# Placing the split weights 16 bytes further on in SBUF, in a two-block float32 transformer kernel

## The chip, the cores and the metric

The kernel runs on one core of a Trainium2 chip. Its time is the device time of one execution in microseconds (us). Lower is better. Three executions were timed.

## The reference

`reference()` computes two blocks on one sequence of 512 tokens and width 1,024, all in float32. The parts that fill the time are the linear layers:

```python
proj = u @ w_in                                   # first block, 1024 -> 2840
h = h + rmsnorm(mixed @ w_out, norm_mix_post)
qx = hn @ w_q_x;  kx, vx = jnp.split(mn @ w_kv_x, 2, axis=-1)
h = h + rmsnorm(ox @ w_o_x, norm_x_post)
g, up = jnp.split(hn @ w_gate_up, 2, axis=-1)     # 1024 -> 2 x 2816
h = h + rmsnorm((silu(g) * up) @ w_down, norm_ffn_post)
...
for l in range(2):                                # second block, two layers of the same kind
    proj = einsum(h, w_in[l]);  ...;  x = x + einsum(merged, w_out[l])
    x = x + (silu(g) * up) @ w_down[l]
```

Between them stand the first block's three attention branches (compressed, selected, window) with a short convolution, a cross-attention to 256 memory tokens, and in each of the two layers of the second block a sliding-window attention with a 31-tap convolution.

## The kernel before

Activations are kept transposed: a tile such as `x_hi` [128, 8, 512] holds feature chunk `k` in its partitions and the 512 tokens along them. Every float32 product of a linear layer is made of three products in `fp32r`, a float32 format that TensorE takes in one pass. Both operands are split in a high part, rounded to fp32r, and a low part, the rest; high x high, low x high and high x low are summed in PSUM. `products` (L406 to L417) issues these three:

```python
pe.matmul(dst, wh[:, k, cols], hi[:, kx_, at:at + width], start=start, stop=False)   # L415
pe.matmul(dst, wh[:, k, cols], lo[:, kx_, at:at + width], start=False, stop=False)   # L416
return pe.matmul(dst, wl[:, k, cols], hi[:, kx_, at:at + width], start=False, stop=stop)  # L417
```

The weights (128 columns) are the stationary operand and are loaded by a weight load (`LDWEIGHTS`, engine PEld) ahead of each matmul. The activations are the moving operand, 512 columns wide, or 256 where a stage works on half the tokens or on the 256 memory tokens. In `tokens_major` (L506 to L516) it is the other way round: the activations are loaded and the weights move, 256 columns wide.

The weights come as a stream of 183 units of 128 x 2048 float32 (8 KiB per partition). Three slots take turns. For each unit SyncE issues a DMA into `w_raw` (L662), ScalarE copies it rounded into `w_hi` (`split_hi`, L293 to L297), VectorE writes `w_raw - w_hi` into `w_lo` (`split_lo`, L299 to L302), and TensorE runs its 48 matmuls. ScalarE waits for the matmuls of the unit three before (`unit_done`), VectorE for ScalarE (`hi_ready`), TensorE for VectorE (`lo_ready`), and the DMA of a slot for VectorE's reading of it. The order of each engine's work is written out by hand.

The attention stages use plain float32 matmuls (for example `kx,qx` at L1570), in which no tile of this stream takes part. Two small stages use fp32r with a narrower stationary operand: the gates (L836 to L838, 24 columns of `wg_hi`/`wg_lo`, moving `x_hi`/`x_lo`), and the compression (L877 to L879, 62 columns of `xc_hi`/`xc_lo`, moving `w_hi`/`w_lo`).

**Places in SBUF.** `place` (L110 to L115) gives each tile a start in the partition and moves a cursor on by the tile's size, rounded up to 32 bytes. L130 rounds the cursor up to 128 bytes ahead of the weights:

```python
where[0] = (where[0] + 127) // 128 * 128
w_raw = place("w_raw", [P, SLOTS, UNIT])
w_hi = place("w_hi", [P, SLOTS, UNIT], F32R)
w_lo = place("w_lo", [P, SLOTS, UNIT], F32R)
h = place("h", [P, DT, T])
```

After them come `h`, `x_hi`, `x_lo`, `rbc`, `acc`, `sq`, and then a region (`scope`) that each stage lays out anew: `f_hi`/`f_lo` of the feed-forward layers, `m_hi`/`m_lo` of the memory, `c_hi`/`c_lo` and `o_hi`/`o_lo` of the second block. Their sizes are multiples of 512 bytes, and L212 pads the region so that `cy` (and with it `c_lo`, `o_hi`, `o_lo`) also starts a multiple of 512 bytes from `scope`. So the distance from `w_hi` or `w_lo` to the start of each of x, f, m, c and o, high and low, is a multiple of 512 bytes. Inside the tiles the steps are such multiples too: 2,048 bytes from chunk to chunk of the activations, 1,024 (or 2,048) bytes and 512 bytes inside a unit. Only the narrow operands differ: `wg_hi` and `wg_lo` are read in steps of 96 bytes, `xc_hi` and `xc_lo` start at 96 bytes past a multiple of 128 and are read in steps of 248 bytes. A line of 16 bytes holds four float32.

Of the kernel before, what the change touches and what calls it, by code (L numbers as in the profile page):

```python
# [23 lines left out]
F32R = mybir.dt.float32r  # L24
# [6 lines left out]
P = 128  # L31
# [16 lines left out]
LOW = -1e20  # L48
SLOTS = 3
UNIT = 2048  # L50


U_IN, U_W1, U_OUT, U_KV, U_QX, U_OX, U_GU, U_DN, U_L = 0, 11, 15, 19, 27, 31, 35, 57, 69
# [47 lines left out]
def build(nc, w, x, mem, pos, pack, tables, cmask, w2, wg, rope2, out):  # L101
    ctx = ExitStack()
    with ctx:
# [6 lines left out]
        def place(name, shape, dt=F32, cursor=where):  # L110
            size = int(np.prod(shape[1:])) * (2 if dt == BF16 else 4)
            t = nc.alloc_sbuf_tensor_at(name, shape, dt, offset=cursor[0])
            cursor[0] += (size + 31) // 32 * 32
            assert cursor[0] <= nc.sbuf_usable_end, (name, cursor[0])
            return t  # L115
# [13 lines left out]
        jcol = place("jcol", [P, 64])  # L129
        where[0] = (where[0] + 127) // 128 * 128  # L130
        w_raw = place("w_raw", [P, SLOTS, UNIT])
        w_hi = place("w_hi", [P, SLOTS, UNIT], F32R)
        w_lo = place("w_lo", [P, SLOTS, UNIT], F32R)
        h = place("h", [P, DT, T])
        act_at = [where[0]]
        y_ffn = place("y_ffn", [P, DT, T], F32, act_at)
# [144 lines left out]

        HALF = UNIT // 2
        QUARTER = UNIT // 4
        FIRST_GAINS = 8
# [2352 lines left out]
def unit_pack(weight, cols, rows=8):  # L2637
# [4 lines left out]
    for c in range(0, k, rows):  # L2642
        u = np.zeros((P, rows, UNIT // rows), np.float32)
        m = min(rows, k - c)
# [114 lines left out]
```

## Time and profile before

| | us |
|---|---|
| median of 3 runs | 2248.32 |
| lowest and highest run | 2246.68, 2249.13 |
| span of the profiled execution, first to last instruction | 2246.4 |
| TensorE busy in it | 2224.9 |
| TensorE weight loads busy | 1821.7 |
| VectorE busy | 1245.1 |
| ScalarE busy | 885.6 |
| GpSimd busy | 280.7 |

The page gives no separate device time for the profiled execution; its span is 1.9 us below the median of the timed runs. Matmuls are pipelined: a matmul's record lasts longer than the distance to the next one's start, so the mean duration of a matmul is not what it costs. What it costs is the distance from start to start, called its pitch below, which is read from the timeline. The granted TensorE clock has two levels, 1.2 and 2.4 GHz. A stream of 512 columns at one column per cycle takes 213.3 ns at 2.4 GHz, one of 256 columns 106.7 ns.

### The profile page before, as it was taken

What the parts mean: (1) busy time and instruction counts of PE and PEld (TensorE: products, weight loads), DVE (VectorE), ACT (ScalarE), POOL (GpSimd) and SP (SyncE); (2) the same over time, 40 slices, a digit from 0 to 9 for tenths busy, and PEclk for the clock granted to TensorE, in tenths of its full rate; (3) what the DMA queues carried; (4) which work ended last, traced back from release to release, by engine and by line L of the source; (5) the groups of instructions that cost most, each with busy time, mean ns of one, the idle gap of its engine ahead of it and who ended that gap; (6) DMA issues with size and microseconds to landing.
All of it is one profiled execution on the core that took longest, in us unless ns stands there. A gap on an engine that the chain in (4) does not pass through costs nothing.

```text
span 2246.4 us, 29245 instructions
## 1 busy us (share of the span) xinstructions
PE 2224.9 (99%) x11388; PEld 1821.7 (81%) x11388; DVE 1245.1 (55%) x1836; ACT 885.6 (39%) x1363; POOL 280.7 (12%) x273
## 2 busy tenths in 40 slices
PE   9999999999999999999999999999999999999999
PEld 7877888898888888886778888888887668888887
DVE  6467656445444225999664444333889664544422
ACT  5545454354333225234744333222323753433321
POOL 3000032011000001014331000001003442000000
PEclk9999999999999999999999999999999999999999
DMA  6221033122222231321122222222221112322222
GB/s 223 100 76 57 20 121 126 55 72 99 103 102 93 94 113 69 113 75 57 56 77 81 107 93 93 100 106 105 104 84 57 39 66 85 113 102 104 94 101 86
DMA packets 30484, 203.19 MB, mean 90 GB/s; under 512 B 3504, under 2 KB 4144, under 8 KB 6704
## 3 DMA queue, kind: packets, MB, share of 16 engines
q1 hardware_dynamic: 29088, 197.34, 24.4%
q10 hardware_dynamic: 1296, 4.46, 0.5%
q8 instruction: 69, 1.13, 0.2%
q14 instruction: 31, 0.25, 0.0%
HBM read 199.69 MB, written 2.10 MB: 90 GB/s over the span
## 4 chain that ended last, share of the span: by engine, by line
PE 93%; DVE 3%; POOL 1%; ACT 1%; issue 1%; DMA 0%; ACTq 0%; DVEq 0%; POOLq 0%
PE bank L415 26%; PE bank L417 26%; PE bank L416 26%; PE bank L2110 1%; PE bank L1002 1%; PE bank L2120 1%; PE bank L2133 1%; PE bank L973 1%; PE bank L2028 1%; POOL acc L324 1%; PE bank L990 1%; PE bank L2010 1%; PE bank L1593 1%; PE bank L1570 1%; PE bank L515 1%
## 5 line engine op out<-in xcount | busy, mean ns | idle before, releaser
L415 PE MATMUL bank<-x_hi,w_hi 128*128 128x512 f32 (+1 forms) x2032 | 789.9, 389 | 5.9 <-DVE x_lo L1766 2.3
L417 PE MATMUL bank<-x_hi,w_lo 128*128 128x512 f32 (+1 forms) x2032 | 775.0, 381 | 0.0
L416 PE MATMUL bank<-x_lo,w_hi 128*128 128x512 f32 (+1 forms) x2032 | 774.1, 381 | 0.0
L301 DVE TENSOR_TENSOR w_lo<-w_raw,w_hi 128x2048 fp32r<-128x2048 f32 x167 | 386.2, 2313 | 412.3 <-ACT w_hi L297 412.3
L297 ACT ACTIVATE w_hi<-w_raw 128x2048 fp32r<-128x2048 f32 x167 | 319.7, 1916 | 585.8 <-PE bank L417 583.9
L415 PEld LDWEIGHTS bank<-x_hi,w_hi 128*128 128x128 f32 x2032 | 382.1, 188 | 83.6 <-issue 6.8
L417 PEld LDWEIGHTS bank<-x_hi,w_lo 128*128 128x128 f32 x2032 | 381.9, 188 | 74.9
L416 PEld LDWEIGHTS bank<-x_lo,w_hi 128*128 128x128 f32 x2032 | 382.4, 188 | 72.7 <-issue 2.9
L415 PE MATMUL bank<-f_hi,w_hi 128*128 128x512 f32 (+1 forms) x572 | 213.3, 373 | 0.0
L416 PE MATMUL bank<-f_lo,w_hi 128*128 128x512 f32 (+1 forms) x572 | 213.2, 373 | 0.0
L417 PE MATMUL bank<-f_hi,w_lo 128*128 128x512 f32 (+1 forms) x572 | 213.2, 373 | 0.0
L2345 DVE SCALAR_TENSOR_TENSOR cy<-la,gains,cy 128x512 f32<-128x512 f32 x240 | 173.9, 794 | 0.0
L563 DVE TENSOR_TENSOR bank<-bank,rbc 128x512 f32<-128x512 f32 x66 | 46.0, 697 | 167.6 <-PE bank L417 159.6
L415 PEld LDWEIGHTS bank<-f_hi,w_hi 128*128 128x128 f32 x572 | 107.7, 188 | 19.0
L416 PEld LDWEIGHTS bank<-f_lo,w_hi 128*128 128x128 f32 x572 | 107.7, 188 | 18.9
L417 PEld LDWEIGHTS bank<-f_hi,w_lo 128*128 128x128 f32 x572 | 107.7, 188 | 18.7
L324 POOL TENSOR_TENSOR acc<-acc,sq 128x512 f32<-128x512 f32 (+1 forms) x48 | 77.6, 1618 | 144.2 <-ACT sq L308 140.4
L552 ACT ACTIVATE f_hi<-bank 128x512 f32 x66 | 39.6, 599 | 115.5 <-DVE bank L569 115.5
L571 DVE TENSOR_TENSOR f_lo<-bank,f_hi 128x512 f32 x66 | 45.7, 692 | 58.4 <-ACT f_hi L552 58.4
L2590 POOL TENSOR_TENSOR lprob<-lprob,small 128x512 f32<-128x512 f32 (+1 forms) x64 | 61.9, 967 | 123.6 <-DVE small L2419 77.8
L2260 ACT ACTIVATE lprob<-lprob,small 128x257 f32<-128x257 f32 (+1 forms) x128 | 60.5, 475 | 31.5 <-DVE small L2415 30.9
L324 POOL TENSOR_TENSOR acc<-sq 128x512 f32<-128x512 f32 (+1 forms) x8 | 14.4, 1801 | 442.8 <-ACT sq L308 442.8
(355 smaller groups left out, 2637.2 us busy)
## 6 DMA issues: line engine op xcount, KB each, us to landing
w_raw<-w_d SPq DMA_DIRECT2D x184, 1024.0 KB, 4.8
out_d<-h SPq DMA_DIRECT2D x8, 256.0 KB, 6.6
h<-x_d ACTq DMA_DIRECT2D x3, 512.0 KB, 9.2
tab<-rope_d ACTq DMA_DIRECT2D x2, 640.0 KB, 3.9
memT<-mem_d ACTq DMA_DIRECT2D x1, 1024.0 KB, 4.8
w_raw<-w_d SPq DMA_DIRECT2D x2, 256.0 KB, 4.1
h<-x_d ACTq DMA_DIRECT2D x2, 256.0 KB, 5.8
w_raw<-w_d SPq DMA_DIRECT2D x1, 512.0 KB, 6.6
```

Of the source, the lines that this page charges most:

```text
L297: act.activation(w_hi[:, u.slot, :], w_raw[:, u.slot, :], ACT.Copy).then_inc(hi_ready, 1)
L301: dve.tensor_tensor(w_lo[:, u.slot, :], w_raw[:, u.slot, :], w_hi[:, u.slot, :], ALU.subtract).then_inc(lo_ready, 1)
L324: pool.tensor_tensor(acc[:, 0:width], sq[:, 0, 0:width] if k == 1 else acc[:, 0:width], sq[:, k % 2, 0:width], ALU.add).then_inc(acc_ready, 1)
L415: pe.matmul(dst, wh[:, k, cols], hi[:, kx_, at:at + width], start=start, stop=False)
L416: pe.matmul(dst, wh[:, k, cols], lo[:, kx_, at:at + width], start=False, stop=False)
L417: return pe.matmul(dst, wl[:, k, cols], hi[:, kx_, at:at + width], start=False, stop=stop)
L552: act.activation(pick(f_hi, j, i), up, ACT.Copy).then_inc(f_hi_done, 1)
L563: dve.tensor_tensor(g, g, rbc[:, :], ALU.mult).then_inc(gu_scaled, 1)
L571: dve.tensor_tensor(pick(f_lo, j, i), up, pick(f_hi, j, i), ALU.subtract).then_inc(f_lo_done, 1)
L2260: act.activation(row, row, ACT.Exp, bias=asm(j, 0, e), scale=-1.0, accum_out=asm(j, 4, e)).then_inc(A["exp"], 1)
L2345: dve.scalar_tensor_tensor(out=cy[:, m, :], in0=src, scalar=wt, in1=cy[:, m, :], op0=ALU.mult, op1=ALU.add).then_inc(l_tap, 1)
L2590: pool.tensor_tensor(row, row, asm(j, 12).unsqueeze(2).to_broadcast([P, 2, 2 * P - c0]), ALU.mult).then_inc(A["scaled"], 1)
```

## The change

`w_hi` and `w_lo` become views of one tile, `w_split`, that begins where `w_hi` began and has four unused float32 (one line of 16 bytes) ahead of them. No instruction is added, removed or moved; only start addresses differ.

```diff
+LINE = 4
...
         w_raw = place("w_raw", [P, SLOTS, UNIT])
-        w_hi = place("w_hi", [P, SLOTS, UNIT], F32R)
-        w_lo = place("w_lo", [P, SLOTS, UNIT], F32R)
+        w_split = place("w_split", [P, LINE + 2 * SLOTS * UNIT], F32R)
+        w_hi, w_lo = (w_split[:, LINE + i * SLOTS * UNIT:LINE + (i + 1) * SLOTS * UNIT].rearrange("p (s c) -> p s c", s=SLOTS) for i in range(2))
         h = place("h", [P, DT, T])
```

`w_hi` and `w_lo` start 16 bytes later than before. `w_split` is 49,168 bytes long, rounded up to 49,184, so that `h` and all tiles after it start 32 bytes later. `w_raw` and what is ahead of it stay. The distance from the split weights to x, f, m, c and o becomes a multiple of 512 bytes plus 16. Distances among the tiles after `w_split` stay as they were, those between `wg_hi`/`wg_lo` and `x_hi`/`x_lo` among them.

## Rows read from the trace of the kernel before

**Rows 1.** The page: span, TensorE's share, and its granted clock in 40 slices.
```profile
span 2246.4 us, 29245 instructions
PE 2224.9 (99%) x11388; PEld 1821.7 (81%) x11388; DVE 1245.1 (55%) x1836; ACT 885.6 (39%) x1363; POOL 280.7 (12%) x273
PEclk9999999999999999999999999999999999999999
```

**Rows 2.** The page's chain that ended last, by engine and by line.
```profile
PE 93%; DVE 3%; POOL 1%; ACT 1%; issue 1%; DMA 0%; ACTq 0%; DVEq 0%; POOLq 0%
PE bank L415 26%; PE bank L417 26%; PE bank L416 26%; PE bank L2110 1%; PE bank L1002 1%; PE bank L2120 1%; PE bank L2133 1%; PE bank L973 1%; PE bank L2028 1%; POOL acc L324 1%; PE bank L990 1%; PE bank L2010 1%; PE bank L1593 1%; PE bank L1570 1%; PE bank L515 1%
```

**Rows 3.** Groups by line and form, TensorE: count | busy us, mean ns | idle before.
```profile
L415 PE MATMUL bank<-x_hi,w_hi 128*128 128x512 f32 x1872 | 743.6, 397 | 3.6 <-DVE w_lo L301 2.0 <-DVE x_lo L406 1.4
L415 PE MATMUL bank<-f_hi,w_hi 128*128 128x512 f32 x484 | 188.3, 389 | 0.0
L415 PE MATMUL bank<-o_hi,w_hi 128*128 128x512 f32 x128 | 51.1, 399 | 0.0
L415 PE MATMUL bank<-x_hi,w_hi 128*128 128x256 f32 x160 | 46.3, 289 | 2.3 <-DVE x_lo L1766 2.3
L415 PE MATMUL bank<-c_hi,w_hi 128*128 128x512 f32 x64 | 27.5, 430 | 0.0
L415 PE MATMUL bank<-f_hi,w_hi 128*128 128x256 f32 x88 | 25.1, 285 | 0.0
L415 PE MATMUL bank<-m_hi,w_hi 128*128 128x256 f32 x64 | 18.3, 285 | 0.0
L514 PE MATMUL bank<-w_hi,m_hi 128*128 128x256 f32 x64 | 18.1, 283 | 0.0
L514 PE MATMUL bank<-w_hi,x_hi 128*128 128x256 f32 x32 | 9.4, 295 | 0.0
```

**Rows 4.** Timeline, TensorE, 512 columns in the feed-forward stage: start us, duration us.
```profile
699.63 0.39 PE L417 MATMUL bank<-x_hi,w_lo 128*128 128x512 f32 x1
...
701.90 0.39 PE L415 MATMUL bank<-x_hi,w_hi 128*128 128x512 f32 x1
```

**Rows 5.** Timeline, TensorE, 256 columns of the down projection.
```profile
829.73 0.28 PE L416 MATMUL bank<-f_lo,w_hi 128*128 128x256 f32 x1
...
830.93 0.28 PE L417 MATMUL bank<-f_hi,w_lo 128*128 128x256 f32 x1
```

**Rows 6.** Timeline, TensorE, plain float32 matmuls of the cross-attention, eight merged.
```profile
404.71 1.89 PE L1570 MATMUL bank<-kx,qx 128*128 128x256 f32 x8
```

**Rows 7.** Timeline, TensorE, 512 columns between attention work in the second block.
```profile
1101.33 0.39 PE L416 MATMUL bank<-c_lo,w_hi 128*128 128x512 f32 x1
...
1103.63 0.39 PE L417 MATMUL bank<-c_hi,w_lo 128*128 128x512 f32 x1
```

**Rows 8.** Timeline, TensorE, the gates: 24 stationary columns, 512 moving.
```profile
74.01 0.39 PE L836 MATMUL bank<-x_hi,wg_hi 128*24 128x512 f32 x1
...
75.85 0.40 PE L838 MATMUL bank<-x_hi,wg_lo 128*24 128x512 f32 x1
```

**Rows 9.** Timeline, TensorE, the compression: 62 stationary columns, 256 moving.
```profile
91.10 0.28 PE L877 MATMUL bank<-w_hi,xc_hi 128*62 128x256 f32 x1
...
92.98 0.28 PE L878 MATMUL bank<-w_lo,xc_hi 128*62 128x256 f32 x1
```

**Rows 10.** The page's groups: the two splits of the weights.
```profile
L301 DVE TENSOR_TENSOR w_lo<-w_raw,w_hi 128x2048 fp32r<-128x2048 f32 x167 | 386.2, 2313 | 412.3 <-ACT w_hi L297 412.3
L297 ACT ACTIVATE w_hi<-w_raw 128x2048 fp32r<-128x2048 f32 x167 | 319.7, 1916 | 585.8 <-PE bank L417 583.9
```

**Rows 11.** The page's DMA issues: KB each, us from issue to landing.
```profile
w_raw<-w_d SPq DMA_DIRECT2D x184, 1024.0 KB, 4.8
out_d<-h SPq DMA_DIRECT2D x8, 256.0 KB, 6.6
h<-x_d ACTq DMA_DIRECT2D x3, 512.0 KB, 9.2
```

## The prediction

> **What bounds the kernel now.** I read the page first. TensorE is busy for 2224.9 of the 2246.4 us and its granted clock is at the upper level, 2.4 GHz, in all 40 slices [rows 1]. The chain that ended last is 93% TensorE, 78% in the three lines of `products` alone [rows 2]. So the kernel is a row of matmuls, and what the change is worth is what it does to their pitch, nothing else of size.
>
> Then I counted the matmuls that read `w_hi` or `w_lo`, from the groups by form [rows 3]. Each of the groups shown stands for three of equal count (high x high, low x high, high x low). With 512 moving columns: (1872 + 484 + 128 + 64) x 3 = 7,644. With 256: (160 + 88 + 64 + 64 + 32) x 3 = 1,224.
>
> Then the pitches, from the timeline; a pitch is the distance of the two starts shown divided by the steps between them.
> - 512 columns, feed-forward: ten steps from 699.63 to 701.90, 227 ns [rows 4]. The stream of columns itself takes 213.3 ns, so 13.7 ns are extra.
> - 256 columns: ten steps in 1.20 us, 120 ns [rows 5], against 106.7: 13.3 extra. The extra does not grow with the columns.
> - Plain float32, the same 128 x 128 weight load ahead of each: eight matmuls in 1.89 us, of which the last lasts 0.38, so seven steps of 216 ns [rows 6]. It streams 256 columns at half the rate, 213.3 ns: 2.7 extra. So a weight load can hide almost fully where the moving operand is read at half the speed.
> - 512 columns right behind attention work: ten steps from 1101.33 to 1103.63, 230 ns [rows 7], by the same instructions at the same distances in SBUF as in rows 4. The pitch has a steady value of 227 and a restless one of 230.
>
> The extra of 11 ns over the float32 case is what the change can reach. 7,644 x 11 + 1,224 x 10.6 = 97 us is all of it, 4.3% of the span.
>
> **The change part by part.** *Removed or added:* no instruction, no wait, no byte of traffic. *Moved:* addresses.
>
> (a) The splits. ScalarE writes `w_hi`, VectorE reads it and writes `w_lo`, at 16 bytes off the old places. 1.92 and 2.31 us per unit [rows 10], both with hundreds of us of idle time ahead, ended by TensorE and by each other: a unit's 48 matmuls take 48 x 0.227 = 10.9 us. Cost 0; it would take a doubling of both to come near that cover, and if the cover went TensorE would wait for `w_lo`. Only the first units lie open: below 1 us either way.
>
> (b) The DMAs. `w_raw` does not move. `h` does, by 32 bytes: its loads (9.2 us to landing) and the eight stores of the result (6.6 us) [rows 11]. Only the last store lies open at the end. If it were a tenth slower or faster that is 0.7 us; I take 0.
>
> (c) The pitch. The trace has no stage with 128 stationary columns and any other distance than a multiple of 512 bytes, so this is bounded by the nearest rows. Below: all of the extra over the float32 case, -97 us by the count above. With 256 columns I doubt it: a load follows every 120 ns there and is busy 160 ns on the mean (1821.7 us over 11,388 [rows 1]), so the loads may set the pace. I keep -88 us, that is 11 ns on the 7,644 and 3 ns on the 1,224 (the step from rows 5 to rows 9). Above: the pitch where the distances are not multiples of 512. The gates, stationary operand in steps of 96 bytes, make eight steps in 1.84 us, 230 ns [rows 8]; the compression, steps of 248 bytes, sixteen in 1.88 us, 117.5 ns [rows 9]. Both have fewer stationary columns too, so they cannot tell the distance from the width.
>
> What I take: rows 9 are nearest, since a quarter of their loads begin an odd number of lines from the moving weights (2 x 248 bytes is 31 lines). They run 2.5 ns below rows 5, and nowhere near 109. So I take 2.5 ns off the 1,224 at 256 columns, -3.1 us. For 512 columns no row shows a gain. Between -11 (rows 6) and +3 (rows 8) I take -0.83 ns, one period of the lower clock level, as an estimate near the present value: -6.4 us. Sum: -9.5 us.
>
> Here a rule speaks against the change. The rows say that something that the float32 case does not feel costs fp32r 11 ns. The Trainium skill ("TensorE: Matmul & The Clock Gate", Part 2, step 1) says that TensorE has two independent SBUF read ports and that loading the next weights takes no read bandwidth from the running matmul; by it there is nothing between the two streams that an address could part, and the term would be 0. This trace neither shows nor excludes it.
>
> **The sum.** 2246.4 - 9.5 = 2236.9 of span. The timed median stands 1.9 us above the span, so 2238.8; I write 2239.
>
> **The rivals.**
> - *Addresses do nothing* (the change doesn't do what its distances are for). The 13 ns would be a fixed cost of fp32r. For: the extra is the same at 256 and at 512 columns, and the gates, which load 24 columns instead of 128, pay no less [rows 5, 8]. Against: 227 and 230 at the same addresses [rows 4, 7] show that the extra is no constant. Time: 2248, give or take 2. The rule of the skill above belongs here.
> - *The steady state is lost, slower.* Place: every 512-column matmul. The steady 227 is seen only where all distances are multiples of 512 bytes; with the 16 bytes the streams might never settle, as in rows 8. Price: 230 - 227 = 3 to 4 ns on 7,644, less about a tenth that runs so already: 21 to 28 us; less 3.1 us for the 256-column ones: +18 to +25, 2266 to 2273. It decides as soon as the share of 512-column matmuls at 230 or more passes one half. For: the gates' 24 matmuls and the compression's never settle. Against: both also differ in width.
> - *The streams part fully.* Weight loads and moving operand got in each other's way at equal lines, and one line of distance ends it: 216 ns and 117. Time 2248.3 - 88 = 2160. For: the 11 ns between rows 4 and 6, and that fp32r reads at twice the rate. Against: the odd quarter of rows 9 shows no such drop. Engines would follow: 48 x 0.216 = 10.4 us a unit against 2.3 for the slower split and 4.8 for the DMA.
> - *A middle case* of a few ns, 3 to 6, on the 512 columns: 2200 to 2225. It shares the reasons of the last one.
>
> **How the numbers follow.** A difference of about 0.2% (4.5 us) is what a measurement of this kernel can tell from none. Chances: my forecast, a small gain down to 2228, 0.26; middle case 0.10; full parting 0.11; nothing 0.23; steady state lost 0.30. Of the forecast some 0.02 ends within 0.2%. So faster 0.45, same 0.25, slower 0.30. The likeliest single figure of a gain is 2239, and its own range 2228 to 2246; cases of both signs hold most of the chance. The range for 8 in 10 has to take in the middle case and the lost steady state: 2190 to 2273. It leaves out the full parting and a pitch worse than that of the restless stages.
>
> **What would show it.** Right: in the feed-forward timeline ten steps take 2.26 us or a little less instead of 2.27, ten 256-column steps about 1.18 instead of 1.20; the groups of L415 to L417 shrink alike in x, f and o; the counts, the splits' means and the DMA rows stay. `kx,qx` stays at seven steps of 216, as its distances did not change. Wrong: ten steps in 2.30 (steady state lost), in 2.16 (full parting), or 2.27 and 1.20 unchanged. Also wrong would be a change at the gates, L836 to L838, whose operands keep their distances, or a change of idle time ahead of TensorE.

## The result, and the profile after

| | before | after |
|---|---|---|
| median of 7 runs each, us | 2248.15 | 2253.94 |
| lowest and highest run | 2246.62, 2249.36 | 2252.0, 2258.22 |
| span of the profiled execution | 2246.4 | 2251.9 |

The ratio of the times is 1.0032, with an interval of 1.0021 to 1.0043. The change makes the kernel slower by about 0.3%. The forecast was 0.4% faster; 2253.94 lies inside the range that was given.

In the changed kernel the three lines of `products` are L416 to L418, the splits L298 and L302, and both weight tiles bear the name `w_split`. First the page: its head, TensorE's share, the granted clock in 40 slices, the chain that ended last by engine, and the groups of the two splits with the DMA issues.

```profile
span 2251.9 us, 29245 instructions
PE 2231.0 (99%) x11388; PEld 1822.6 (81%) x11388; DVE 1245.2 (55%) x1836; ACT 885.3 (39%) x1363; POOL 280.7 (12%) x273
PEclk9999999999999999999999999999999999999999
...
PE 93%; DVE 3%; POOL 1%; ACT 1%; issue 1%; DMA 0%; ACTq 0%; DVEq 0%; POOLq 0%
...
L302 DVE TENSOR_TENSOR w_split<-w_raw,w_split 128x2048 fp32r<-128x2048 f32 x167 | 386.4, 2314 | 412.2 <-ACT w_split L298 412.2
L298 ACT ACTIVATE w_split<-w_raw 128x2048 fp32r<-128x2048 f32 x167 | 319.8, 1917 | 590.7 <-PE bank L418 588.8
...
out_d<-h SPq DMA_DIRECT2D x8, 256.0 KB, 6.4
h<-x_d ACTq DMA_DIRECT2D x3, 512.0 KB, 8.8
```

Against [rows 1, 2, 10, 11]: the same counts of instructions, the same chain, the splits 1 ns longer each, the DMAs of `h` 0.2 and 0.4 us shorter. What grew is TensorE's busy time, 6.1 us for 5.5 us of span. So the difference lies in what TensorE itself takes for the same work, and the timeline of TensorE (start us, duration us, line) is where to look. It stands here for four stages, each answering to one group of before: the first block's feed-forward (in the second block the same stage follows below it), the 256-column down projection, the matmuls between attention work, and plain float32.

```profile
699.65 0.39 PE L416 MATMUL bank<-x_hi,w_split 128*128 128x512 f32 x1
...
701.92 0.39 PE L417 MATMUL bank<-x_lo,w_split 128*128 128x512 f32 x1
...
1299.70 0.39 PE L416 MATMUL bank<-x_hi,w_split 128*128 128x512 f32 x1
...
1301.98 0.39 PE L417 MATMUL bank<-x_lo,w_split 128*128 128x512 f32 x1
...
829.51 0.28 PE L416 MATMUL bank<-f_hi,w_split 128*128 128x256 f32 x1
...
830.68 0.28 PE L417 MATMUL bank<-f_lo,w_split 128*128 128x256 f32 x1
...
1101.24 0.40 PE L417 MATMUL bank<-c_lo,w_split 128*128 128x512 f32 x1
...
1103.54 0.39 PE L418 MATMUL bank<-c_hi,w_split 128*128 128x512 f32 x1
...
405.74 1.89 PE L1571 MATMUL bank<-kx,qx 128*128 128x256 f32 x8
```

Ten steps each: 2.27 us in the first feed-forward, as in [rows 4]; 2.28 in the second block's; 1.17 at 256 columns, where [rows 5] have 1.20; 2.30 in the restless stage, as in [rows 7]; the float32 row is that of [rows 6]. A difference of 1 ns in a step is at the edge of what ten steps show. Many steps show it surely. Here are equal stretches inside the first feed-forward and the two of the second block, TensorE alone, before the change (window, its length, TensorE busy and its count of matmuls, granted clock, DMA share, GB/s):

```profile
560.00:800.00 240.00, 240.00 (x1060) 1.00 0.28 100
1260.00:1540.00 280.00, 280.00 (x1237) 1.00 0.28 101
1940.00:2220.00 280.00, 280.00 (x1237) 1.00 0.29 103
```

The same three stretches after it:

```profile
560.00:800.00 240.00, 240.00 (x1060) 1.00 0.28 99
1260.00:1540.00 280.00, 280.00 (x1228) 1.00 0.28 98
1940.00:2220.00 280.00, 280.00 (x1228) 1.00 0.28 98
```

In the first stretch nothing changed. In each of the other two 9 matmuls fewer fit into 280 us: the settled pitch is 228.3 ns there and 226.7 in the first, by the same instructions and the same distances between the tiles. That is the core of this case.

**Where the 5.5 us come from.** Both kernels issue the same 11,388 matmuls in the same order, so each distance from start to start can be set against its partner:

```
kind of matmul                  count   before -> after, mean ns   sum, us
split stream, 512 columns       7,400       227.29 -> 227.98          +5.2
  the same, pitches over 245 ns    243                                +1.9
split stream, 256 columns       1,314       120.73 -> 119.05          -2.2
  the same, long ones                                                 +0.4
all others                                                            +0.3
span                                                                  +5.5
```

(The parts are rounded. The 256-column row takes in the compression.) Over the run, the second block's two feed-forward stages cost 2.2 and 2.4 us, the rest of the second block another 1 us, and the 256-column stages give 1.8 us back (0.3 by 90 us, 0.8 between 234 and 517, 0.8 between 772 and 868). Two places are not the pitch but the granted clock. At 513 us it fell to its lower level for 3.4 us, which cost 1.6 us. At 223 us it fell in both kernels, for 3.4 us before the change and 6.8 us after it, which cost 0.6 us net (a wait of 0.87 us for ScalarE's `prob` that came next before the change is gone after it); this is inside the "all others". So some 2.2 of the 5.5 us came with the clock, and the rest is the pitch's. The page's 40 slices are too coarse to show a fall. Windows around the two places show them, after the change (all of TensorE alone, columns as above):

```profile
222.00:232.00 10.00, 10.00 (x53) 0.66 0.17 51
510.00:517.00 7.00, 6.04 (x25) 0.76 0.18 47
```

Before the change, the same windows:

```profile
222.00:232.00 10.00, 9.80 (x62) 0.83 0.09 28
510.00:517.00 7.00, 6.14 (x34) 1.00 0.07 11
```

Is the whole loss then the clock's? The mean granted clock of the timed runs says no. Where it is 1.000, which a fall of 3.4 us would bring to 0.999, the spans are 2250.0 and 2250.0 us here and 2248.3 and 2252.2 in experiment 4, against 2244.8 to 2245.9 in six runs of the kernel before. The loss without a fall is 2 to 7 us.

### The profile page after: what moved, and what is told of

It reads as the page before. It is cut to its first block, busy times and chain, and to the rows that moved or that the text cites. A ratio compares the mean times of both kernels' runs of the same rounds, so it can differ in the third digit from the quotient of the medians.

```text
span 2251.9 us, 29245 instructions
## 1 busy us (share of the span) xinstructions
PE 2231.0 (99%) x11388; PEld 1822.6 (81%) x11388; DVE 1245.2 (55%) x1836; ACT 885.3 (39%) x1363; POOL 280.7 (12%) x273
## 4 chain that ended last, share of the span: by engine, by line
PE 93%; DVE 3%; POOL 1%; ACT 1%; issue 1%; DMA 0%; ACTq 0%; DVEq 0%; POOLq 0%
PE bank L416 27%; PE bank L417 26%; PE bank L418 26%; PE bank L1003 1%; PE bank L2111 1%; PE bank L2121 1%; PE bank L2134 1%; PE bank L974 1%; PE bank L991 1%; PE bank L2029 1%; POOL acc L325 1%; PE bank L2011 1%; PE bank L1594 1%; PE bank L1571 1%; PE bank L517 0%
## 5 line engine op out<-in xcount | busy, mean ns | idle before, releaser
L416 PE MATMUL bank<-x_hi,w_split 128*128 128x512 f32 (+1 forms) x2032 | 791.3, 389 | 6.1 <-DVE x_lo L1767 2.6
L417 PE MATMUL bank<-x_lo,w_split 128*128 128x512 f32 (+1 forms) x2032 | 776.3, 382 | 0.0
L418 PE MATMUL bank<-x_hi,w_split 128*128 128x512 f32 (+1 forms) x2032 | 776.2, 382 | 0.0
L302 DVE TENSOR_TENSOR w_split<-w_raw,w_split 128x2048 fp32r<-128x2048 f32 x167 | 386.4, 2314 | 412.2 <-ACT w_split L298 412.2
L298 ACT ACTIVATE w_split<-w_raw 128x2048 fp32r<-128x2048 f32 x167 | 319.8, 1917 | 590.7 <-PE bank L418 588.8
L416 PEld LDWEIGHTS bank<-x_hi,w_split 128*128 128x128 f32 x2032 | 382.2, 188 | 85.5 <-issue 6.8
L418 PEld LDWEIGHTS bank<-x_hi,w_split 128*128 128x128 f32 x2032 | 382.0, 188 | 75.5
L417 PEld LDWEIGHTS bank<-x_lo,w_split 128*128 128x128 f32 x2032 | 382.4, 188 | 73.6 <-issue 2.9
L416 PE MATMUL bank<-f_hi,w_split 128*128 128x512 f32 (+1 forms) x572 | 213.6, 373 | 0.0
L418 PE MATMUL bank<-f_hi,w_split 128*128 128x512 f32 (+1 forms) x572 | 213.5, 373 | 0.0
L417 PE MATMUL bank<-f_lo,w_split 128*128 128x512 f32 (+1 forms) x572 | 213.4, 373 | 0.0
L417 PEld LDWEIGHTS bank<-f_lo,w_split 128*128 128x128 f32 x572 | 107.4, 188 | 19.5
L416 PEld LDWEIGHTS bank<-f_hi,w_split 128*128 128x128 f32 x572 | 107.4, 188 | 19.5
L418 PEld LDWEIGHTS bank<-f_hi,w_split 128*128 128x128 f32 x572 | 107.4, 188 | 19.3
```

The source lines that it names most:

```text
L298: act.activation(w_hi[:, u.slot, :], w_raw[:, u.slot, :], ACT.Copy).then_inc(hi_ready, 1)
L302: dve.tensor_tensor(w_lo[:, u.slot, :], w_raw[:, u.slot, :], w_hi[:, u.slot, :], ALU.subtract).then_inc(lo_ready, 1)
```

## The experiments

The theory after the result: the pitch of an fp32r matmul depends on where the stationary and the moving tile lie to each other, and a place can have more than one steady pitch; the new place has a worse one beside that of before. The rivals: the addresses do nothing by themselves, and the difference is the 32-byte shift of `h` and what follows, or a disturbance that came with it; or an odd number of lines is good, and something else eats its gain.

Five kernels measure the pitch by itself. They compute no part of the model. They hold one pair of fp32r tiles (and one of plain float32), and issue sections of mostly 96 matmuls (48 in the map) in this kernel's order of high and low parts and its steps inside the tiles, nearly every section behind three float32 matmuls. Only the start of the tiles, the width, the type or what goes ahead differs from section to section. The lines shown are cut from each kernel's list of sections. A section's values are: a name, the bytes by which the stationary and the moving tile are moved, stationary columns (`P` is 128), bytes from one stationary slice to the next, moving columns, type, number of matmuls, and columns of the three matmuls ahead (the sweep has no such value). In the rows that follow a section's matmuls are merged to one row: the mean pitch is its duration, less the 0.39 us that the last record lasts (0.28 at 256 columns), divided by 95. The settled pitch that I quote is read from the single starts of a section's later part. "Stationary on an even line" means a start at a multiple of 32 bytes, "on an odd line" 16 bytes past one. Before, the weights lay on an even line at distance 0 (modulo 256); the change puts them on an odd line, with the activations 16 bytes further on (modulo 256): `h` and what follows moved by 32 bytes, the weights by 16.

**1. A sweep of the distance.** 32 sections, the moving tile 16 bytes further on each time.

```diff
+    for j in range(32):
+        yield ("d" + "abcdefghijklmnopqrstuvwxyzABCDEF"[j], 0, 16 * j, P, 512, 512, F32R, 96)
```

> No part of the model is computed: 32 sections of 96 fp32r matmuls each (128 stationary, 512 moving columns, high and low parts in the kernel's order), in which the moving tile starts a multiple of 512 bytes from the stationary one plus 0, 16, 32, ... 496 bytes. Theory A (the distance sets the pitch): section 0 settles at 226.7 ns; section 1 (16 bytes) at 228.3 ns; the others differ from one another, with the same figure at distances that are alike modulo some power of two. Theory B (what counts is where the moving tile lies against 64 or 128 bytes, not the distance): the pattern repeats every 4 or 8 sections and the multiples of 128 bytes all give 226.7. Theory C (addresses do nothing, the pitch hangs on how the first matmul falls): all 32 sections within 0.3 ns of one another, or scattered without order.

The timeline, one row a section: distances 0, 16, 32, 64, 240 and 256.

```profile
40.00 22.04 PE L86 MATMUL bank<-xfill,wfill 128*128 128x512 f32 x96
62.46 22.49 PE L90 MATMUL bank<-xfill,wfill 128*128 128x512 f32 x96
85.37 22.64 PE L86 MATMUL bank<-xfill,wfill 128*128 128x512 f32 x96
...
131.50 22.23 PE L86 MATMUL bank<-xfill,wfill 128*128 128x512 f32 x96
...
384.53 22.95 PE L90 MATMUL bank<-xfill,wfill 128*128 128x512 f32 x96
407.91 22.03 PE L86 MATMUL bank<-xfill,wfill 128*128 128x512 f32 x96
```

(22.04 - 0.39) / 95 = 228 ns at distance 0, (22.95 - 0.39) / 95 = 237 at 240. The settled pitches are 226.7, 231.7, 233.3, 228.9 and 236.7 at 0, 16, 32, 64 and 240, and the sixteen values from 256 bytes on repeat the first sixteen. So the place matters, by up to 10 ns, its period is 256 bytes, and distance 0 is the best of the row. Addresses do something, and nothing of what they do here is a gain.

**2. Widths, and the place of both.** Both tiles moved, starts inside a line, 256 columns, fewer stationary columns, plain float32.

```diff
+    for dw, dx in ((0, 0), (0, 16), (16, 32), (16, 16), (32, 32), (64, 64), (16, 0)):
+        yield ("both", dw, dx, P, 512, 512, F32R, 96, P)
+    for dx in (4, 8, 12):
+        yield ("inside a line", 0, dx, P, 512, 512, F32R, 96, P)
+    for dw, dx in ((0, 0), (0, 16), (16, 32), (0, 32), (0, 64), (0, 128), (0, 256), (0, 496)):
+        yield ("half width", dw, dx, P, 512, 256, F32R, 96, P)
+    for cols, step, width in ((24, 512, 512), (24, 96, 512), (64, 512, 512), (96, 512, 512), (62, 512, 256), (62, 248, 256)):
+        yield ("narrow", 0, 0, cols, step, width, F32R, 96, P)
+    for dx in (0, 16):
+        yield ("plain", 0, dx, P, 512, 256, F32, 48, P)
+    for dx in (0, 16):
+        for ahead in (16, 32, 48, 64, 96, 112):
+            yield ("ahead", 0, dx, P, 512, 512, F32R, 96, ahead)
```

> No part of the model is computed: sections of 96 matmuls. Both tiles moved by 0/0, 0/16, 16/32, 16/16, 32/32, 64/64, 16/0 bytes: theory A gives 226.7 for equal moves and one other figure, 228.3, for 0/16 and 16/32; theory B gives 226.7 only for 0/0 and 64/64 or for none but 0/0. Half width (256 moving columns): 120 at distance 0 and 117.4 at 16 under A, 120 everywhere under C. Narrow stationary operands at distance 0: if the width makes the 230 ns of the gates, 24 columns in steps of 512 bytes run at 230 like those in steps of 96; if the distance makes it, the first run at 226.7. Plain float32: 216 at distance 0 and 16 under all theories. The last twelve sections repeat distances 0 and 16 behind matmuls of six different widths: A with one steady state gives one figure for each distance; with two steady states the sections at 16 bytes split into 226.7 and 228.3 and those at 0 all stay at 226.7.

The timeline of this kernel: 24 stationary columns in steps of 512 and of 96 bytes, 62 of them in steps of 512 and of 248 bytes at 256 moving columns, and plain float32 at distances 0 and 16 (one source matmul in float32 makes two records).

```profile
363.36 22.44 PE L98 MATMUL bank<-xfill,wfill 128*24 128x512 f32 x96
386.22 22.39 PE L102 MATMUL bank<-xfill,wfill 128*24 128x512 f32 x96
...
454.54 11.17 PE L98 MATMUL bank<-xfill,wfill 128*62 128x256 f32 x96
...
466.13 11.48 PE L102 MATMUL bank<-xfill,wfill 128*62 128x256 f32 x96
...
478.11 20.89 PE L98 MATMUL bank<-xplain,wplain 128*128 128x256 f32 x96
499.50 20.89 PE L102 MATMUL bank<-xplain,wplain 128*128 128x256 f32 x96
```

- 512 columns, stationary/moving moved by: 0/0 226.7; 32/32 and 64/64 the same; 16/16 230.0; 0/16 231.7; 16/0 233.3; **16/32, the place of the change, 226.7.** So not only the distance counts, but also whether the pair sits on an even or an odd line.
- Starts inside a line: 237.9 at 4 bytes, 232.8 at 8, 228.9 at 12.
- 256 columns: 120 at 0, 128 and 256; 118.7, 116.7, 117.8 and 117.1 at 16, 32, 64 and 496; 117.3 at the place of the change.
- 62 stationary columns, the compression's, at 256 moving columns and distance 0: 113.3 in steps of 512 bytes, 117.1 in the compression's own steps of 248.
- 24 columns: 231.1 and 230.8, whatever the step; 230.0 with 64 or 96. The gates' 230 of [rows 8] is thus the price of few stationary columns, not of their distances.
- Plain float32: 215.8 at both places.
- Behind matmuls of six other widths, 0/0 stays at 226.7 and 0/16 at 231.6 to 231.7: one steady pitch each.

By this run the change should have cost nothing at 512 columns and gained 2.7 ns at 256, which is nearly what was forecast. It is not what the kernel did, so a second thing was missing.

**3. The neighbours' 32 bytes alone,** in the model's kernel: the weights stay, `h` and all that follows move by 32 bytes.

```diff
         w_lo = place("w_lo", [P, SLOTS, UNIT], F32R)
+        where[0] += 32
         h = place("h", [P, DT, T])
```

> The whole kernel with the weights where they were before and h and all behind them 32 bytes further on, so that the distance is two lines instead of one and everything but the weights lies as in the changed kernel. If the odd line is the cause: steady pitch 226.7 or at least not 228.3, and a time within 0.1% of before. If moving x, f, m, c and o off their 128-byte places is the cause: like the changed kernel, 0.2 to 0.4% slower, with 228.3 in the second block's feed-forward layers. If addresses do nothing: ratio 1.000.

2291.04 us, ratio 1.0193 (1.0176 to 1.021). Timeline, and the stretch of the first feed-forward:

```profile
699.73 0.40 PE L416 MATMUL bank<-x_hi,w_hi 128*128 128x512 f32 x1
...
702.07 0.40 PE L417 MATMUL bank<-x_lo,w_hi 128*128 128x512 f32 x1
...
560.00:800.00 240.00, 240.00 (x1030) 1.00 0.26 93
```

This is none of the three times that were expected. Ten steps in 2.34 us; over the run 512 columns go from 227.3 to 233.25 ns (+44.2 us) and 256 columns give 1.7 us back. The sweep gave 233.3 for this distance, so the small kernels carry over to the large one. And the change is seen to hold two moves: the 32 bytes by which it pushes the activations, dear by themselves, and the 16 bytes on the weights, which take nearly all of that back.

**4. The change again,** unedited, for its spread and its stages.

> The changed kernel once more. If the loss is made by the addresses: 2250 to 2258 again, with 228.3 ns steady in some stages and 226.7 in others, perhaps in other stages than in the first profile, as the choice between two steady states would hang on timing. If it was made by this chip's dips of the granted clock alone: within 0.1% of before, where as many dips show.

2253.95 us (2250.36 to 2257.89, nine runs), ratio 1.0025 (1.0015 to 1.0036). Its profiled execution repeats the first one's stages: 226.7 in the first feed-forward, 228.3 in the second block's, and a span of 2251.9. The three stretches:

```profile
560.00:800.00 240.00, 240.00 (x1060) 1.00 0.28 98
1260.00:1540.00 280.00, 280.00 (x1228) 1.00 0.27 98
1940.00:2220.00 280.00, 280.00 (x1228) 1.00 0.28 98
```

In both profiled executions the same stages have the same pitch, and the clock falls at the same two places. That the choice is the same in every execution is not shown: at a mean granted clock of 1.000 the spans of the change's timed runs go from 2248.3 to 2252.2 us, those of the kernel before from 2244.8 to 2245.9, so something beside the clock varies there that was not profiled.

**5. A map of all places.** 16 x 16 sections of 48: both tiles at every line of 256 bytes.

```diff
+    for i in range(16):
+        for j in range(16):
+            yield ("map", 16 * i, 16 * j, P, 512, 512, F32R, 48, P)
```

> No part of the model is computed: 256 sections of 48 fp32r matmuls (128 stationary, 512 moving columns), the stationary tile moved by 16 times 0 to 15 bytes, the moving tile by 16 times 0 to 15 bytes. Theory A1 (the distance alone, modulo 256 bytes): the map is constant along its diagonals. That is against what the last run showed at 16/16 (230.0) beside 0/0 (226.7). Theory A2 (the distance, and for each distance whether the stationary tile lies on an even or an odd line): the map repeats when both are moved by 32 bytes, so that 256 sections hold 32 different figures, among them 226.7 at 0/0, 16/32 and everything 32 bytes from these, 231.7 at 0/16, 233.3 at 0/32 and 16/0. If an odd distance were good in itself, the 128 sections with one would be lower on the mean than the 128 with an even one; A2 gives no such order. A figure below 226.7 anywhere would be a place that beats both kernels.

The pattern repeats when both tiles move by 32 bytes, so two rows hold it. Settled pitch in ns by the distance; each entry was met in eight sections, and where two values stand, both were:

```
distance           0      16     32     48     64     80     96     112
even line        226.7  231.7  233.3  233.3  228.9  231.1  233.3  231.1/226.7
odd line       230-233  226.7  232.2  232.0  226.7  230.0  233.4  233.3
                       /228.3 /233.3 /233.3
distance          128    144    160    176    192    208    224    240
even line        232.2  233.3  234.2  233.3  233.3  234.6  233.3  236.7/233.3
                /233.4               /231.1
odd line         233.3  233.3  226.7  232.0  228.8  233.3  226.7  233.3
                              /230.0        /233.3
```

Three things. Nothing lies below 226.7: the kernel before already had the best pitch there is. "An odd number of lines" is no rule: over all places the odd distances have a mean of 232.3, the even ones 231.1. And the place of the change (odd line, 16) is one of those with two steady pitches, 226.7 in seven sections and 228.3 in one.

**6. What picks the pitch.** The two places, each entered behind matmuls of different widths.

```diff
+    for dw, dx in ((0, 0), (16, 32)):
+        for ahead in (16, 32, 48, 64, 80, 96, 112, 128):
+            yield ("ahead", dw, dx, P, 512, 512, F32R, 96, ahead)
+    for dw, dx in ((0, 0), (16, 32), (0, 0), (16, 32)):
+        for cols in (128, 62, 24, 96):
+            yield ("behind narrow", dw, dx, cols, 512, 256, F32R, 24, P)
+            yield ("then full", dw, dx, P, 512, 512, F32R, 96, 0)
+    for cols in (8, 32):
+        for dx in (0, 16, 32, 64, 128, 240):
+            yield ("few columns", 0, dx, cols, 512, 512, F32R, 72, P)
```

> No part of the model is computed: sections of 96 matmuls. The places of before (0/0) and of the change (16/32), each behind matmuls of eight widths and then behind fp32r matmuls with 128, 62, 24 and 96 stationary columns and 256 moving ones. If the changed places have two steady states and the entry chooses: the sections at 0/0 all end at 226.7, those at 16/32 partly at 226.7 and partly at 228.3. If the 228.3 in the changed kernel comes from other engines' work and not from the entry: all at 226.7 here. Few stationary columns (8 and 32) at six distances: if the stationary load's reading is what disturbs the moving one, 8 columns (two lines) should stand near 216 at every distance; if the start of each matmul costs it, the figures stay near 230 whatever the columns.

The timeline, at the place of the change, behind widths of 16 and of 32 columns:

```profile
219.63 22.18 PE L95 MATMUL bank<-xfill,wfill 128*128 128x512 f32 x96
...
242.24 22.03 PE L99 MATMUL bank<-xfill,wfill 128*128 128x512 f32 x96
```

22.18 against 22.03 is 0.15 us over 95 steps: 228.3 against 226.7. The matmuls ahead differ, the section does not. At the place of the change six of the eight sections behind widths settled at 228.3; behind fp32r matmuls of 62 stationary columns it was 228.3, behind 128, 24 and 96 it was 226.7, the same both times. At the old place every section settled at 226.7. Both pitches last until the section ends. The three matmuls ahead are not the whole entry: behind three of 128 columns this place settled at 228.3 here, but at 226.7 in experiment 2 and in seven of the eight sections of the map, where other sections stood before them. The same kernel holds sections with few stationary columns: with 8, the pitch is 231.1 at distance 0, 235.6 at 16, 231.6 at 64 and 228.8 at 240; with 32, 231.7, 232.0, 231.6 and 228.9. With 128 columns it is 226.7, 231.7, 228.9 and 236.7 at these distances. So a load of 8 columns, a sixteenth of the data, is dearer at three of the four and cheaper at 240, and it never comes near 216.

**7. The map at 256 columns,** and two more places at 512 (16/80 and 16/240, odd line, distances 64 and 224) with many entries.

```diff
+    for dw in (0, 16):
+        for j in range(16):
+            yield ("half width", dw, dw + 16 * j, P, 512, 256, F32R, 96, P)
+    for dw, dx in ((16, 80), (16, 240)):
+        for ahead in (16, 32, 48, 64, 80, 96, 112, 128):
+            yield ("ahead", dw, dx, P, 512, 512, F32R, 96, ahead)
+    for dw, dx in ((0, 0), (16, 32), (16, 80), (16, 240)):
+        for cols in (128, 62, 24, 96):
+            yield ("behind narrow", dw, dx, cols, 512, 256, F32R, 24, P)
+            yield ("then full", dw, dx, P, 512, 512, F32R, 96, 0)
+    for ahead in (16, 32, 48, 64, 80, 96, 112, 128):
+        yield ("half ahead", 0, 0, P, 512, 256, F32R, 96, ahead)
+        yield ("half ahead", 16, 32, P, 512, 256, F32R, 96, ahead)
```

> No part of the model is computed: the 32 places of the map (stationary tile on an even or an odd line, distance 0 to 240 bytes) at 256 moving columns, and then how steady four of them are. If the extra at half width follows the same order as at full width: 120 at distance 0, more elsewhere. The trace of the changed kernel and earlier sections say otherwise (120 at 0, 118.7, 117.3 and 116.7 at other places), so I expect nearly all places between 113 and 120 and distance 0 among the worst. Of 16/80 and 16/240, where the map has 226.7 at full width, each behind eight widths: if they have one steady state, as 0/0, all sixteen sections end at 226.7 and such a place would lose nothing at full width while it gains at half width; if two, as 16/32, they split.

The timeline at 0/0 and at 16/80:

```profile
40.06 11.76 PE L98 MATMUL bank<-xfill,wfill 128*128 128x256 f32 x96
...
280.01 11.13 PE L98 MATMUL bank<-xfill,wfill 128*128 128x256 f32 x96
```

The best places at 256 columns have a settled pitch of 113.3 ns: even line at 112 and 192, odd line at 64 and 192. The old place has 120.0, and the map has nothing higher than 120.1. The place of the change has two again, 120.0 and (in six of the eight sections behind widths) 117.3. At 512 columns both added places stood at 226.7 in all 24 sections. An odd line at distance 64 is thus the one place that was best at both widths in every section here with 128 stationary columns.

**8. Distance 64 on an even line,** in the model's kernel.

```diff
-        where[0] = (where[0] + 127) // 128 * 128
+        where[0] = (where[0] + 63) // 64 * 64
...
         w_lo = place("w_lo", [P, SLOTS, UNIT], F32R)
+        where[0] += 64
```

> The whole kernel with all behind the weights 64 bytes further on (the weights begin at a multiple of 64 instead of 128 bytes, to make room): distance 64, stationary tile on an even line. If the map of places holds in the kernel: 228.9 ns at 512 columns instead of 226.7, 2.2 x 7,400 = +16 us, less 2.2 x 1,300 = 3 us at 256: 2257 to 2264. If any distance that is no multiple of 256 bytes costs what 32 bytes cost: 2291.

2260.3 us, ratio 1.0055 (1.0039 to 1.007). Timeline in the second block's feed-forward:

```profile
1299.77 0.39 PE L418 MATMUL bank<-x_hi,w_lo 128*128 128x512 f32 x1
...
1302.06 0.39 PE L416 MATMUL bank<-x_hi,w_hi 128*128 128x512 f32 x1
```

Ten steps in 2.29, 228.9 settled: +16.6 us at 512 columns (2.9 of it in pitches over 245 ns; the clock fell for 3.4 us at 513 and at 885 us). 256 columns fall from 120.7 to 116.6 ns: -5.4. The sum, 11.2, is the difference of the spans (2257.6 against 2246.4), as the rest cancels. The same move with the rounding left at 128 did not fit into the partition and has no time; the first line of the edit makes the room. A better place for the narrow stage is no better for the kernel when the wide one pays.

**9. Three lines instead of one.** The change with 32 bytes more: an odd line still, an odd distance still, 48.

```diff
         w_split = place("w_split", [P, LINE + 2 * SLOTS * UNIT], F32R)
+        where[0] += 32
         h = place("h", [P, DT, T])
```

(The rounding ahead of `w_raw` is 64 here too; with 128 this one did not fit either and has no time.)

> The changed kernel with all behind the weights another 32 bytes on: the weights on an odd line as in the change, the distance 48 bytes, again an odd number of lines (and the weights' start at a multiple of 64 instead of 128 bytes plus 16). If an odd number of lines is what keeps the changed kernel near 2254: 2250 to 2258 again. If the map holds (231.8 or 233.3 at this place): +5 to +6.6 ns on 7,400 matmuls against before, less 2 us: 2283 to 2295.

2280.57 us, ratio 1.0142 (1.0126 to 1.0157), a span of 2280.9; that is 2.4 us below the time that the map was expected to give. The same three stretches:

```profile
560.00:800.00 240.00, 240.00 (x1031) 1.00 0.26 93
1260.00:1540.00 280.00, 280.00 (x1209) 1.00 0.27 94
1940.00:2220.00 280.00, 280.00 (x1209) 1.00 0.29 101
```

233.3 ns in the first and 231.8 in the other two, both of them values of the map for this place (+37.0 us at 512 columns, -3.0 at 256). This ends the rival that an odd distance helps in itself: the change with another odd distance is 1.4% slower than before, not 0.3%.

**10. Odd line, distance 64,** the place that experiment 7 points to, for w with x, f and m; c and o end up 80 off. The high and the low part of each pair share a tile with a 16-byte line ahead, and small tiles move to make up 64 bytes.

```diff
+        def place_pair(name, a, b, cursor=where):
+            n = a * b
+            t = place(name, [P, LINE + 2 * n], F32R, cursor)
+            return (t[:, LINE + i * n:LINE + (i + 1) * n].rearrange("p (a b) -> p a b", a=a) for i in range(2))
...
+        w_hi, w_lo = place_pair("w_split", SLOTS, UNIT)
+        eps_c = place("eps_c", [P, 3])
         h = place("h", [P, DT, T])
...
+        x_hi, x_lo = place_pair("x_split", DT, T)
...
+        f_hi, f_lo = place_pair("f_split", FT, T, a)
...
+        m_hi, m_lo = place_pair("m_split", DT, MEM, a)
```

> The place that the maps single out: w, x, f and m all on odd lines, the moving ones 64 bytes (modulo 256) from the weights; 226.7 at 512 columns from every entry and 113.3 at 256, and where the weights move (distance 192 from the activations) 113.3 too. c and o stay on even lines 80 bytes off (230.0 in the map). Small tiles change places to make the distances; no instruction differs. If the maps hold in the kernel: 6.7 ns less on some 1,200 matmuls, -8 us, a little less of the restless stretches, 576 matmuls of c and o +3 ns at most, +1 us: 2238 to 2243, ratio 0.995 to 0.998. If half width in the kernel stays at 117 to 120, or other engines' work breaks the steady state: 2245 to 2255.

2244.16 us (2241.55 to 2246.35, eleven runs) against 2248.53, ratio 0.9979 (0.997 to 0.9988). Timeline at 256 columns, and the three stretches:

```profile
828.73 0.28 PE L420 MATMUL bank<-f_split,w_split 128*128 128x256 f32 x1
...
829.87 0.28 PE L421 MATMUL bank<-f_split,w_split 128*128 128x256 f32 x1
...
560.00:800.00 240.00, 240.00 (x1060) 1.00 0.28 99
1260.00:1540.00 280.00, 280.00 (x1237) 1.00 0.28 100
1940.00:2220.00 280.00, 280.00 (x1237) 1.00 0.29 103
```

Ten steps of 256 columns in 1.14 us where [rows 5] have 1.20; 1060, 1237 and 1237 matmuls, as before the change. At 256 columns it gains 5.9 us and loses 1.4 in long pitches, at 512 it gains 1.8 and loses 2.0 in long ones; the span is 4.2 us shorter. It is the one version that is faster than the kernel before, by 0.2%. The expected 2238 to 2243 was missed by 1.2 us: not every stretch of 256 columns runs at 113.3, some of 24 and 48 matmuls run at 118.4 (the 48 that start near 316 us, for one), so in the kernel this place has a second pitch at that width too.

## Why the prediction was wrong

**What bounds the kernel: right.** What TensorE takes for its matmuls, and nothing else of size; the chain by engine is line for line the one of [rows 2].

**(a) The splits cost 0, (b) the DMAs cost 0: right.** 2314 and 1917 ns against 2313 and 1916 in [rows 10], and 0.4 and 0.2 us less for the DMAs of `h`.

**(c) The pitch: this step failed,** in its 512-column term, "I take -0.83 ns". Measured: +0.7 ns on the mean of the 7,400 short ones (+5.2 us where -6.4 was forecast), made up of 0 in the first feed-forward and +1.7 in the second block's two. This term outweighs all others: 7,644 matmuls turn every tenth of a nanosecond into 0.8 us. What stood behind the term was no row but the hope that the 11 ns over plain float32 could be had by parting the streams. The map shows nothing below 226.7 in 256 places. The kernel sat at the optimum for 512 columns, and a step from an optimum is not downwards. A restless 230 beside a steady 227 in the trace of before was there to say that 227 is a good value that can be lost. That 2253.94 lies inside the stated range is the range's width (2190 to 2273, with cases of both signs in it): the forecast's own case ended at 2246.

The 256-column term came out near, by luck: -2.5 ns forecast, -1.7 measured, -2.2 us instead of -3.1. The place has two pitches at this width too, 120.0 and 117.3, so less than the whole difference arrived. But the row it was taken from was misread. The compression's 117.5 was taken for what odd distances give. Experiment 2 takes it apart: with its 62 stationary columns and distances of 512 bytes the pitch is 113.3, with its own steps of 248 bytes 117.1. Against the 120.0 of [rows 5] the narrower operand gains 6.7 ns, and the steps cost 3.8 of them.

**The rival "addresses do nothing": false.** They did up to 10 ns in the sweep, and experiment 3 cost 1.9% by 32 bytes alone. Here the rule that was set against the change has to be weighed. Plain float32 keeps 215.8 ns at both places tried. The Trainium skill ("TensorE: Matmul & The Clock Gate", Part 2, step 1) says that the two operands come through read ports of their own and that a weight load takes nothing from the running matmul; the float32 rows agree with that, and the fp32r rows do not bear out its consequence, that places can't matter: they matter by 10 ns. As to the amount that a load reads: at 512 columns and distance 0 a load of 8 columns gains nothing over one of 128 (231.1 against 226.7), which agrees with the rule, but at 256 columns and distance 0 one of 62 or 24 columns does, 113.3 against 120.0.

**The rival "the steady state is lost": the right mechanism, the wrong size.** The pitch of 226.7 is given up for another in part of the stages. But the other is steady too, and costs 1.7 ns, not 3 to 4; it took hold in the two second-block feed-forwards. The share of 512-column pitches at 230 or over, which the forecast wanted above one half, went from 12% to 14%. Its reason, the gates' 230 in [rows 8], did not hold: with 24 columns the pitch is 231 in steps of 512 bytes as well.

**"The streams part fully" and the middle case: false.** At 512 columns no place came near 216 ns.

**What would show it.** The forecast named 2.26 and 1.18 for right and 2.30 or 2.16 for wrong. The rows came out at 2.27 and 2.28, and 1.17: between the cases, and too near to each other to be told from ten steps. The count of matmuls in an equal stretch tells them apart (1237 and 1228), and that should have been the named sign.

The float32 row (seven steps of 216), the gates (23 steps, mean 231 before and after) and the splits stayed, as was said.

**One more term had no place in the sum: the clock,** 2.2 us. The prediction read "in all 40 slices" at the upper level from the page, but a digit 9 stands for 90% or more of a slice, and a fall of 3.4 us at 223 us was already in the trace of before. In both profiled executions of the change that fall lasted 6.8 us, and another of 3.4 us came at 513 us, as in that of experiment 8. Around 513 us TensorE has waits in both kernels: 0.86 of the 7 us before the change, 0.96 after. Why the clock fell there in one kernel and not in the other is not shown. By the runs at a mean clock of 1.000 this term is not what makes the change slower: 2248.3 to 2252.2 us of span against 2244.8 to 2245.9.

**What stays open.** Shown is that the place sets the pitch, and that at some places the entry picks one of two. Why it is so inside TensorE, with a period of 256 bytes that is neither a tile's size nor a step of this kernel, is not. Nor is what entry the second-block feed-forwards have that the first has not, nor whether the same stages take the slower pitch in the executions that were not profiled. The 13.3 ns between 226.7 and the stream's 213.3 could not be removed by any place; whether they can be otherwise was not tried.

## What to carry to other kernels

A kernel that is bound by TensorE at fp32r has its layout as a tuning knob (32 bytes cost 1.9% here), but a knob with a table and no rule: measure all places of stationary against moving operand in 16-byte lines, modulo 256 bytes, on even and on odd lines, at each width that the kernel uses, and choose by the width that carries the time. When one tile is moved or padded, everything behind it moves too: count that shift as an edit of its own. And look for places with one steady pitch however they are entered; a place that has the best pitch only behind some matmuls is worth less than its table entry.

## What the runs showed of the hardware that was not expected

- The pitch of fp32r matmuls with 512 columns runs from 226.7 to 236.7 ns by place alone (to 237.9 when a tile starts inside a 16-byte line), with a period of 256 bytes in the distance and of 32 bytes in the common place. At 256 columns it runs from 113.3 to 120.0. Plain float32 stands at 215.8 at both places tried.
- The best place of one width is not that of the other: distance 0 on an even line is the best at 512 columns (226.7) and among the worst at 256 (120.0).
- Many settled values differ by multiples of 1.67 ns (226.7, 228.3, 230.0, 231.7, 233.3, 236.7; others, such as 228.9, do not).
- Some places have two steady pitches, 226.7 and 228.3 for that of the change. What ran ahead picks one (more than the three matmuls directly ahead count), and it then lasts for the whole stretch, 280 us of feed-forward in the windows above.
- A narrower stationary operand does not make the pitch shorter at 512 columns: 231.1 ns with 8 or 24 columns, 230.0 with 64 or 96, 226.7 with 128, all at distance 0. At 256 columns and distance 0 it does: 113.3 with 24 or 62 columns, 116.0 with 96, 120.0 with 128.
- The granted clock fell to its lower level for 3.4 or 6.8 us at a time, which 40 slices of a page do not show: at 223 us in the kernel before and in the change, at 513 us in the change only.
